# Both MLP products of a decoder layer as one level of Strassen's algorithm

## The reference

```
h = layer_norm(ALPHA * x + mla_mixer(x, ...), ln_g[0], ln_b[0])       # 512 x 2048, float32
h = layer_norm(ALPHA * h + sq_relu_mlp(h, w1, w2), ln_g[1], ln_b[1])
def sq_relu_mlp(x, w1, w2):                                           # w1 2048 x 8192, w2 8192 x 2048
    return jnp.square(jax.nn.relu(x @ w1)) @ w2
```

## Time and profile before

| what | value |
|---|---|
| median of 3 runs | 2056.19 us (2052.12 to 2059.28) |
| span of the profiled execution | 2053.8 us (its own time: the profile gives none beside the span) |
| PE busy | 1979.3 us, 96% |
| DVE, ACT, POOL busy | 496.6, 596.1, 833.7 us |
| DMA | 195.21 MB, mean 95 GB/s |

### The profile page before, as it was taken

The page is one execution under the profiler, slowest core; times in us unless marked ns, Lnnn a source line. Parts: engine busy times, 40 slices in busy tenths (PEclk is TensorE's granted clock), DMA queues, the critical chain, the costliest instruction groups (busy, mean ns, idle before and its releaser), DMA issues.

```text
span 2053.8 us, 24166 instructions
## 1 busy us (share of the span) xinstructions
PE 1979.3 (96%) x9152; PEld 1653.7 (81%) x9152; DVE 496.6 (24%) x791; ACT 596.1 (29%) x822; POOL 833.7 (41%) x348
## 2 busy tenths in 40 slices
PE   8989999999988999999999999999999999999994
PEld 6868888888877888888888888888888888888883
DVE  2134545521146621111111111111111111111127
ACT  4235545522123222221231222122122222222222
POOL 4232222324432543444344444435444444544443
PEclk9989999999999999999999999999999999999997
DMA  5221111153221232332232233223323323332332
GB/s 208 72 82 62 56 56 51 61 212 106 93 81 63 94 103 91 102 102 93 92 101 97 88 102 102 92 92 102 99 85 102 102 82 102 102 102 82 102 103 82
DMA packets 52452, 195.21 MB, mean 95 GB/s; under 512 B 5952, under 2 KB 5952, under 8 KB 51392
## 3 DMA queue, kind: packets, MB, share of 16 engines
q1 hardware_dynamic: 50976, 185.62, 27.1%
q10 hardware_dynamic: 1440, 9.07, 1.1%
HBM read 190.47 MB, written 4.19 MB: 95 GB/s over the span
## 4 chain that ended last, share of the span: by engine, by line
PE 93%; DVE 5%; ACT 1%; issue 1%; DMA 0%; SPq 0%; DVEq 0%; ACTq 0%
PE bank L734 31%; PE bank L739 30%; PE bank L738 30%; DVE rot L510 1%; ACT swap L285 1%; DVE swap L507 0%; DVE rows L717 0%; PE bank L767 0%; PE bank L978 0%; DMA raw<-weights 0%; DVE rot L506 0%; DVE rows L660 0%; DVE act_lo L665 0%; ACT table L409 0%; DVE act_hi L663 0%
## 5 line engine op out<-in xcount | busy, mean ns | idle before, releaser
L207 POOL TENSOR_TENSOR w_lo<-raw,w_hi 128x1024 fp32r<-128x1024 f32 x338 | 818.3, 2431 | 1190.0 <-ACT w_hi L242 1190.0
L242 ACT ACTIVATE w_hi<-raw 128x1024 fp32r<-128x1024 f32 x338 | 357.0, 1057 | 1190.4 <-PE bank L734 621.7
L734 PE MATMUL bank<-act_hi,w_hi 128*128 128x512 f32 x1168 | 460.7, 394 | 10.5 <-DVE act_lo L471 8.9
L738 PE MATMUL bank<-act_lo,w_hi 128*128 128x512 f32 x1168 | 458.1, 392 | 0.0
L739 PE MATMUL bank<-act_hi,w_lo 128*128 128x512 f32 x1168 | 457.9, 392 | 0.0
L734 PE MATMUL bank<-w_hi,mid_hi 128*128 128x512 f32 (+1 forms) x1152 | 435.4, 378 | 0.0
L738 PE MATMUL bank<-w_lo,mid_hi 128*128 128x512 f32 (+1 forms) x1152 | 434.9, 378 | 0.0
L739 PE MATMUL bank<-w_hi,mid_lo 128*128 128x512 f32 (+1 forms) x1152 | 434.7, 377 | 0.0
L619 DVE SCALAR_TENSOR_TENSOR rows<-rows,bank 128x512 f32<-128x512 f32 x144 | 98.9, 687 | 707.0 <-PE bank L739 707.0
L734 PEld LDWEIGHTS bank<-act_hi,w_hi 128*128 128x128 f32 x1168 | 221.4, 190 | 57.6 <-POOL w_lo L207 8.1
L739 PEld LDWEIGHTS bank<-act_hi,w_lo 128*128 128x128 f32 x1168 | 221.5, 190 | 46.5
(11 more groups left out here) (104 smaller groups left out, 1289.7 us busy)
## 6 DMA issues: line engine op xcount, KB each, us to landing
raw<-weights SPq DMA_DIRECT2D x338, 512.0 KB, 3.3
x_raw<-x_t SPq DMA_DIRECT2D x8, 512.0 KB, 8.5
rows<-x_rows ACTq DMA_DIRECT2D x4, 1024.0 KB, 8.5
ln_rows<-ln ACTq DMA_DIRECT2D x4, 1024.0 KB, 19.4
out_rows<-rows SPq DMA_DIRECT2D x8, 512.0 KB, 2.6
table<-tables ACTq DMA_DIRECT2D x1, 640.0 KB, 3.6
gains<-gains ACTq DMA_DIRECT2D x1, 20.0 KB, 3.4
```

The costliest lines, as they stand in the source:

```text
L207: pool.tensor_tensor(w_lo[:, s, :], raw[:, s % RAWS, :], w_hi[:, s, :].bitcast(f32), ALU.subtract)\
L242: act.activation(w_hi[:, s, :], raw[:, s % RAWS, :], ACT.Copy).then_inc(w_hi_made, 1)
L734: first_pass = pe.matmul(out_, a_hi, b_hi, start=start, stop=False)
L738: pe.matmul(out_, a_hi, b_lo, start=False, stop=False)
```

## The change

The three parts that the change touches are the end of the output projection, the whole MLP and the SBUF places of most buffers. One level of the Winograd form of Strassen's algorithm replaces each of the two products: operands are cut in halves both ways (tokens 0..255 and 256..511), 7 products of half-size blocks replace 8, and sums and differences of blocks are made first on DVE (and a few on POOL).

Up: 32 "pairs" i, each making hidden tiles i and i+32. A pair has 7 steps u of 8 products with 256 tokens moving. SP loads four 128x1024 parts of w1 (b11, b12, b22, b21), DVE makes T1 to T4 from them in place, ACT rounds the 7 results into the four slots, DVE makes 4 of the lo parts and POOL 3. The outputs (4 blocks of 128x256) are put together from PSUM and three kept products, squared, and turned into the 7 left operands of the down product on DVE; their hi and lo go to DRAM (`acts_kept`, 1.8 MB a pair, in runs of 1 KB) from ACT's queue.

Down: 16 "periods" q (8 chunks of 1024 hidden features, by 2 column halves), each of 7 steps s, each step of two 128x1024 weight units n, each unit of 2 token tiles by 2 products of 512 columns. DVE makes T1 to T4 (8 instructions), 7 lo parts, and 14 evictions of 128x512 blocks from PSUM into `acc`; POOL makes 7 lo parts. The left operands come back from DRAM (512 KB a step and chunk), so do the normalised rows (`rows_kept`), from which POOL makes the gained and biased residual in periods 3, 5, 7 and 9 and DVE adds it in periods 4, 6, 8 and 10.

The transposes of rows 0 and 1 now stand ahead of the projection's last row part on PE. The core of the diff, one engine after the other:

```diff
+A22, A11, A12, S1, S2, S3, S4 = range(7)
+STEP_OF = (A11, A12, S2, S1, S3, S4, A22)
+UP_SLOT = (2, 3, 0, 1, 2, 3, 0)
+DOWN_SLOT = (2, 3, 0, 1, 2, 3, 0, 1, 2, 3, 0, 2, 3, 0)
+            def up_loads(i, parity):                                # SP
+                sp.wait_ge(up_lo_pool, 3 * i - 3)
+                load_up(b22[parity], i, 2, b22_loaded[parity])
+                sp.wait_ge(up_lo_pool, 3 * i - 1)
+                load_up(b12, i, 1, b12_loaded)
+                sp.wait_ge(up_t_made, 4 * i)
+                sp.wait_ge(up_lo, 4 * i - 2)
+                load_up(b11, i, 0, b11_loaded)
+                sp.wait_ge(up_lo, 4 * i)
+                load_up(b21, i, 3, b21_loaded)
+            for i in range(UP_PAIRS):                               # POOL
+                up_rest(i, 3)
+                up_rest(i, 5)
+                if i < UP_PAIRS - 1:
+                    up_rest(i + 1, 1)
+            for q in range(PERIODS):
+                for s in range(STEPS):
+                    down_rest(q, s)
+                    if q % 2 and 1 <= q // 2 <= TT and s in (1, 4):
+                        gain_residual(q // 2 - 1, s // 4)
+            def up_pair(i):                                         # ACT, for i > 0
+                c21(i - 1)
+                act.wait_ge(up_t_made, 4 * i + 3)
+                up_weights(i, 2, b11)
+                square_hidden(i - 1)
+                keep_product(i, 0, bank[:, i % 2, :], 1)
+                act.wait_ge(up_t_made, 4 * i + 2)
+                up_weights(i, 3, b12)
+                act.wait_ge(up_t_made, 4 * i + 1)
+                up_weights(i, 4, t3)
+                hidden_hi(i - 1)
+                act.wait_ge(b22_loaded[i % 2], 16 * (i // 2 + 1))
+                up_weights(i, 5, b22[i % 2])
+                keep_product(i, 1, bank[:, i % 2, :], 3)
+                act.wait_ge(up_t_made, 4 * i + 4)
+                up_weights(i, 6, b21)
+                keep_product(i, 2, bank[:, 3, :], 4)
+                store_hidden(i - 1)
...
+                up_weights(i + 1, 0, b11)
+                act.wait_ge(b21_loaded, 16 * (i + 2))
+                up_weights(i + 1, 1, b21)
+            for i in range(UP_PAIRS):                               # DVE
+                if i:
+                    up_rest(i, 2)
+                    hidden_sums(i - 1)
+                    up_rest(i, 4)
+                    hidden_lo(i - 1)
+                if i:
+                    up_t4(i)
+                    dve.wait_ge(h_lo_made, i)
+                c_block(i, 0)
+                if i:
+                    up_rest(i, 6)
+                c_block(i, 1)
+                if i < UP_PAIRS - 1:
+                    up_t3_t1(i + 1)
+                    up_rest(i + 1, 0)
+                    c_block(i, 2)
+                    up_t2(i + 1)
+            def period(q):                                          # DVE
+                if q:
+                    evicts_and_stats(q - 1, 6)
...
+                    down_rest(q, 1)
+                    down_t2(q)
...
+                evicts_and_stats(q, 0)
+                down_rest(q, 2)
+                evicts_and_stats(q, 1)
+                down_rest(q, 3)
+                down_t4(q)
+                evicts_and_stats(q, 2)
+                down_rest(q, 4)
+                evicts_and_stats(q, 3)
+                down_rest(q, 5)
+                if not last:
+                    down_t3(q + 1)
+                evicts_and_stats(q, 4)
+                down_rest(q, 6)
+                if not last:
+                    down_t1(q + 1)
+                    evicts_and_stats(q, 5)
+                    down_rest(q + 1, 0)
+            def up_products(u, parity, ready=None):                 # PE
...
+                for k in range(HK):
...
+                    last = product(dst, w_hi[:, s, cols], w_lo[:, s, cols], a_hi[:, k, :], a_lo[:, k, :],
+                                   u in (0, 1, 3) and k == 0, k == HK - 1, u in (2, 4, 5, 6))
```

More of the change, by code:

```diff
@@ L428, in chunk, with affine @@
[L428 to L437, removed]
+            def affine(n):
+                a, g = n // HK, n % HK
+                act.wait_ge(t_done, n + 1)
+                for k in (2 * g, 2 * g + 1):
+                    last = act.activation(norm_t[:, k, a, :], bank[:, 4 + n % 4, HT * (k % 2):HT * (k % 2) + HT], ACT.Identity,
+                                          scale=gains[:, 8 + k:9 + k], bias=gains[:, 8 + KD + k:9 + KD + k])
+                last.then_inc(t_act, 1)
@@ new lines, in _ @@
+            for t in range(2):
+                finish_row(t)
+            for n in range(1, HK, 2):
+                affine(n)
+            dve.wait_ge(t_act, HK // 2)
+            finish_row(2)
+            left_lo(A11, norm_t[:, :, 0, :], 0, 0)
+            up_rest(0, 0)
+            finish_row(3)
+            up_t3_t1(0)
+            up_t2(0)
+            for n in range(HK + 1, 2 * HK, 2):
+                affine(n)
+            dve.wait_ge(t_act, HK)
+            dve.wait_ge(t_dve, HK)
+            dve.wait_ge(rows_spilled, 16 * TT)
@@ new lines, in measure, with evicts_and_stats, scale_row @@
+            def measure(row, col):
+                dve.bn_stats(stats[:, row, col, :], acc[:, row, 512 * col:512 * col + 512]).then_inc(row_stats, 1)
+            def evicts_and_stats(q, s):
+                evicts(q, s)
+                if q >= PERIODS - 2 and s in (1, 4, 5, 6):
+                    dve.wait_ge(evicted, DOWN_EVICTS * q + 2 * s + 2)
+                    for t in range(2):
+                        measure(t + (0 if s in (1, 5) else 2), column(s, q % 2))
+            def scale_row(t):
+                for half in range(2):
@@ L723, in _ @@
+            for q in range(PERIODS):
+                period(q)
+            last_rows(PERIODS - 1, 5, 0)
+            last_rows(PERIODS - 1, 5, 1)
+            dve.wait_ge(last_gains_loaded, 32)
+            scale_row(1)
+            last_rows(PERIODS - 1, 6, 0)
+            last_rows(PERIODS - 1, 6, 1)
+            scale_row(2)
+            scale_row(3)
         @block.tensor
@@ L1033, in _stream @@
+            for q in range(2):
+                down_period(q, q, 0)
+            with pe.Fori(1, DOWN_CHUNKS - 1) as c:
+                for parity in range(2):
+                    down_period(2 * c + parity, parity, c)
+            for parity in range(2):
+                down_period(PERIODS - 2 + parity, parity, DOWN_CHUNKS - 1, parity == 1)
+def _stream(w_in, w_uq, w_ukv, w_o):
     import numpy as np
```

858 lines of the change are left out of this document (637 added, 221 removed).

## The result

The kernel with the change takes 2113.0 us, median of 4 runs (2109.8 to 2113.5), against 2056.9 (2052.1 to 2059.3): ratio 1.028, 95% interval 1.026 to 1.030. It is slower by 56 us. The forecast was 2066, slower by 9; the value lies in the range, near its upper end. The profiled execution took 2112.6 us with a span of 2110.8.

What follows compares the result with a forecast made beforehand. PE, busy 96% of the span, was taken to bound the kernel before the change. Start 679 + up pairs 688 + passage 3 + down periods 629 + residual 34 + tail 31 = 2064, carried to 2066 us; range 1960 to 2120.

Steps and rivals of the forecast that it cites:

- The start: Everything before the steady up pairs, until DVE starts T2 of pair 1: 679 us, ends 665 and 690.
- PE's passes: Matmul spacing on PE: 0.1195 us for 256 columns in up, 0.2267 for 512 in down; 642 and 609 us.
- DVE and POOL shut each other out: A DVE instruction with two SBUF inputs and a POOL instruction never overlap; 20.5 us of such work an up pair.
- The up pair, 22.2: Steady up stage: DVE's chained order with POOL's parts sets 22.2 us a pair, 31 pairs 688 us.
- rival C: Up stage: loads fall behind the stores once b21 takes over 4.4 us; at 6.5, 24.3 a pair, 2131 us; chance 0.15.
- The down stage: Between up and down 3 us, then 16 periods of 39.3 us making 629, plus 34 for the residual.
- the wait forecast before step 2: Each down period: DVE finishes lo(2) at 12.0 us, PE wants it at 10.9, so late by 1.1 us.
- The residual: Down stage: POOL's gains and DVE's additions exceed PE's period by 5.5 and 3 us, four times: 34 us.
- The tail: After PE's last matmul, four rows stand in DVE's queue: 31 us in place of 27.
- rival D: Up stage: PE's short waits bring its granted clock under 0.97, +1 us a pair, 2097 us; chance 0.08.
- the fast case (B): Up and down: POOL's requests fall into DVE's waits, PE is the bound, pair 20.4, 1971 us; chance 0.30.

Runs made afterwards that it cites:

- E8: Changed kernel with E1, E2, and ACT squaring the hidden blocks before rounding T2, DVE making their sums earlier: 2003.5 us, ratio 0.975.
- E3: Changed kernel with POOL's lo parts of the up product on 32 of 1024 columns (output not the reference's): 1994.9 us, ratio 0.971.
- E1: Changed kernel with b21 of the odd up pairs in a buffer of its own, loaded a pair earlier: 2087.9 us, ratio 1.016.
- E7: Changed kernel storing one of seven down operands a pair, which the down product reads for all seven (output not the reference's): 2048.0 us, ratio 0.995.
- E6: Changed kernel with POOL's gain and bias instructions and DVE's additions of the residual on 16 of 1024 columns: 2080.7 us, ratio 1.011.
- E2: Changed kernel with DVE making T4 ahead of the hidden blocks' lo parts, b21 in its single buffer: 2048.4 us, ratio 0.996.
- E5: Changed kernel with E1 and E2 together: 2051.4 us, ratio 0.999.

## Why the prediction went as it did

**The start**: T2 of pair 1 forecast at 679, measured 677.7. Right.

**PE's passes**: 0.1203 and 0.2265 us (550 / 2428) for 0.1195 and 0.2267. Right: E8 and E3 show the floor.

**DVE and POOL shut each other out**: right. T4's 3.43, the 2.49 of a 256-wide sum asked while POOL runs, and E1's 3.08 for T2 each hold the wait for a POOL instruction. The amount of this work was no bound though: E8 runs it all in 20.15, where the prediction had 20.5. Its prices were durations; DVE's instructions in a row start 1.14 apart at 1024 columns and 0.34 at 256, and with POOL's least of 2.35 the same list comes to 8 x 1.14 + 4 x 0.34 + 2.0 + 3 x 2.35 = 19.5.

**The up pair, 22.2**: here is the step that failed, by 1.6 us a pair and 50 in all. What was said of DVE and POOL holds in sum (17.6 measured for 17.8). What failed is the load of b21, for which the sum took no more than 4.4 us: it takes 6.2 beside the stores on the mean, and 3.9 without most of them (E7). That is rival C, given 0.15. Its argument against had a right number, for the stage moves 167 GB/s on the mean where 177 was reckoned, but it is the wrong one: the requests come together, and in the load's own flight the engines are full (1.04 and 1.05). That the loads stand in another queue than the stores did not protect the load. What the prediction cited of the Trainium skill ("DMA: Bandwidth & Descriptors", "Specifications"), that 512 B reach line rate, the trace doesn't contradict: with 1 KB runs among them the transfers go at 363 to 402 GB/s, and at 335 in E7 with fewer. But a rate says nothing of how many bytes share it with a load, and the rule was used as if it did. This speaks for the stores' bytes and not their 1 KB runs as the cause; runs of another size were not tried.

The load explains the 1.6 us of this kernel; it doesn't follow that a cure of it gives them back. E1 takes the load out of the circle and a pair is still 23.1, since POOL's parts then fall on other instructions.

**The down stage**: 3 + 629 + 34 forecast, 664 measured from the end of up to PE's last matmul. Right in sum, by two errors, which is luck. A plain period is 38.1 and not 39.3: the wait forecast before step 2 is not there. This gave back 19 us. They were lost at the stage's beginning, of which the sum had only 3 us; the first period takes 59.4, 21 over the plain one:

```profile
1429.80 0.76 PE L1284 MATMUL bank<-w_hi,down_act 128*128 128x512 f32 x1 [8.21 <-issue]
...
1445.43 0.77 PE L1284 MATMUL bank<-w_hi,down_act 128*128 128x512 f32 x1 [8.01 <-DVE w_lo L1092]
```

```profile
1409.13 0.58 ACTq L672 DMA_DIRECT2D acts_kept<-h_lo  x1
...
1438.28 1.70 ACT L664 ACTIVATE h_hi<-hidden 128x1792 fp32r<-128x1792 f32 x1 [6.36 <-DMA acts_kept<-h_lo]
```

PE (first fence) waits twice for 8 us. The first wait ends with DVE's lo(1), which ends at 1429.69. By the order of the queues, ACT waited 3.2 us for down weights, its squares stood behind that rounding, and DVE's sums and lo(1) behind the squares; no run isolates it. ACT (second fence) shows the second wait's source: the last pair's operands may be written only when the store of the pair before has landed. That store, asked at 1409.13, took 29.1 us (the median is 10.9), so until 1438.2. From 1408.6 to 1438.2 the DMA share is 0.95 to 1.02, with the first loads of the down stage asked behind the store. DVE's hidden lo, and lo(2) behind it in the queue, waited 8.0 us for it. E7, whose stores are a seventh, has the first wait still (7.6) and not the second, and this is the rest of its gain. After the two waits PE's first 9 and 12 matmuls stand 0.43 us apart in place of 0.2267, some 4.5 us more in all; the granted clock from 1440 to 1450 is 0.53, so mostly its lower level, 1.2 GHz. In the up stage a store has a pair's time to land. A cure was not tried.

**The residual**: 34 forecast, 32 measured (E6). (Its sum had a slip: 43.9 is 5.8 over 38.1 and not 5.5, which makes 35.) **The tail**: PE's last matmul 2079.7, end 2110.8: 31, as forecast. **The clock** (rival D): the granted clock was 0.97 over the up stage, at the bound that the prediction had set, 0.92 in one window and 1.00 in another, with pairs of 24.0 and some 23.7 us. Were that difference all the clock's, it would be 0.3 us in the slower pairs, where D had put 1.

The sum with what was measured: 678 + 738 + 664 + 31 = 2111, the span. So the direction and, in sum, every part but one were right; the slowdown came out six times the forecast, since one term of 31 repetitions was 1.6 us short. That the other parts add up so closely owes something to the two errors of the down stage. The chances had the fast case (B) at 0.30; E8 shows it is real, but behind an order of instructions that the change doesn't have.

## What to carry to other kernels

Where a stage repeats, write down the closed circle of one repetition, from the release of a buffer through its load back to the release, and give the load the time that it has beside the stores of that stage, not its median over the page: add up the bytes that are asked for together with it, and look at the DMA share in a window cut to its flight, not in the mean of the stage. Where a circle of in-order queues binds, price an edit only together with the others: the same second buffer was worth 0, 25 or 77 us here, and one moved line 65. Before cutting shared work of DVE and POOL, look which instruction POOL falls upon, and who waits for that one; T4 cost 2 us a pair until it went one place forward (E2), and cost them again once b21 came early (E5).

## What the hardware showed unexpectedly

A 512 KB load took 6.2 us on the mean from request to use beside two stores of 896 KB, and 3.9 beside two of 128 KB. The mean DMA share of the stage, 0.46 in one window, hid that the engines were full in just these microseconds (1.04 and 1.05, at 363 and 402 GB/s). The lo stores of 896 KB in 1 KB runs took from 4.7 to 29.1 us. PE ran for 450 us without a gap (E8) while DVE was busy 97% of the same time, its waits for POOL included.
